# Forgetting attention: the forget sums of the row maxima, subtracted on VectorE inside the reduction instead of added by a TensorE pass

## The chip, the core and the metric

One program runs on one core of a Trainium2 chip. The metric is the device time of one execution in microseconds. All inputs and outputs are in device memory. The numbers are f32; matrix products marked fp32r read f32 operands in the rounded form that the kernel makes by a copy ("hi"), with the rest kept in a second tile ("lo").

## The reference, cut to what matters

The program is one inference step of a two-layer decoder (a gated-linear-attention layer, then a forgetting-attention layer) for a prompt of 2048 tokens and eight single-token samples. The change touches the prompt's forgetting attention alone: 16 heads of 64, causal.

```python
f_all = jnp.cumsum(logf, axis=1)                       # F, one value per token and head
...
s = jnp.einsum('bqhd,bkhd->bhqk', q_blk, k_all)        # q already scaled
s = s + fq_blk.transpose(0, 2, 1)[..., None] - f_k[:, :, None, :]
s = jnp.where((kpos[None, :] <= qpos[:, None])[None, None], s, -jnp.inf)
p = jax.nn.softmax(s, axis=-1)
return jnp.einsum('bhqk,bkhd->bqhd', p, v_all)
```

F of the query is the same for all keys of a row and falls out of the softmax. What is needed is q.k - F(key), its maximum over each query's keys, the exponential of the difference, the sum, and the product with V.

## The kernel before

The kernel is a row of phases, each a block in which every engine has its own instruction stream and waits on semaphores; the order on each engine is the order of the code. The phase of the change is `attention_phase` (L1316 to L1906). The phases ahead of it (modulation, projections, linear attention) and behind it (the samples' attention, the output projection) are not touched.

**Work of a pair.** Two heads share the 128 partitions, 64 each, so there are 8 pairs (`PAIRS`); `step(j, u)` is the work of one pair on an engine and `run_steps` (L1453) runs the eight, six of them in a loop whose body holds two. Queries are cut in 4 groups G of 512, keys in 16 tiles of 128.
- *Logits.* For each group G and key tile i there is one unit e, 40 per pair (`exp_units`). TensorE writes keys x queries of both heads into one of two pairs of PSUM banks: hi by hi, hi by lo, lo by hi, and a fourth product of the tiles `k_more` and `q_more`, whose rows add -F of the key and minus the query's maximum (L1631). ScalarE takes the exponential (L1732), GpSimd adds it to the running sum (L1898), TensorE multiplies it by V (`weigh_v`, L1651).
- *Maxima.* They must be known first, so they are made ahead in the other layout, queries x keys: also 40 units per pair, one for each query tile t and block c of up to 512 keys (`maxima`, L1598). Each is a hi by hi product of both heads, 64 rows each, and a second product of the constant tile `pick_f` (ones in the two rows where `k_more` holds -F in two parts) and `k_more`, which adds -F of the key to every row of the sum (L1602). The unit on the diagonal (c = t // 4) also gets two small bf16 products that write the causal mask, and is 128, 256, 384 or 512 wide. VectorE then takes the maximum of both heads by one TENSOR_REDUCE (L1774).
- All maxima units use one pair of banks (`bank_max`), so TensorE may write the next one only when VectorE has read the last (`max_done`, L1596).

**The order.** `slots_of` gives each unit e of a pair its extras: one maxima unit per slot (slots 0 to 15 the last query group of the same pair, slots 16 to 39 the first three groups of the next pair), and at some slots a transposition of q or k (`turn`), the row of maxima (`m_row`), the sums (`sum`, 16 tiny products) or the reciprocal's transposition (`spread`). In a slot TensorE does (`unit`, L1665): the wait and mask of the unit's logits; for a diagonal maxima unit its wait for `max_done` and its mask; the logits; for any other maxima unit its wait; the maxima; V times the exponentials of the unit before; the slot's extra. VectorE has in each slot the maximum, then the extra's part, then in eight slots (`page_at`) one half of the scoring of a cache page of a sample (a multiplication of 1024 columns at L1797, a reduction at L1800). Before the eight steps stand the first 24 maxima of pair 0 (`first_slots`), with two sets of banks in turn.

**The forget sums** are scanned on VectorE once (`forget_sums`, L1833) into `F`, 16 partitions of 2048, split in -F hi and lo, stored to `f_both` and loaded from there per pair into two rows of `k_more` (`load_f`).

Of the kernel before, what the change touches and what calls it, by code (L numbers as in the profile page):

```python
# [11 lines left out]
P = 128  # L12
# [1303 lines left out]
def attention_phase(nc, g):  # L1316
# [11 lines left out]
    maxima_of = lambda G: [("max", t, c) for t in range(R * G, R * G + R) for c in range(G + 1)]  # L1328
    ahead = [f for G in range(NG - 1) for f in maxima_of(G)]
    AHEAD = len(ahead)  # L1330
    max_slots = list(enumerate([(OWN, f) for f in maxima_of(NG - 1)] + [(NEXT, f) for f in ahead]))
# [35 lines left out]
    page_at = (1, 5, 10, 15, 20, 27, 33, 38)  # L1367
    PT = 5
    with ExitStack() as st:
# [6 lines left out]
        pick_f = sb("pick_f", [P, P], F32R)  # L1376
# [7 lines left out]
        o_raw, spread, o = ([sb(f"{n}{s}", [P, NB]) for s in range(2)] for n in ("o_raw", "spread", "o"))  # L1384
# [13 lines left out]
        v_loaded = [sem(f"v_loaded{u}") for u in range(2)]  # L1398
        turn_full, turn_hi, turn_used = sem("turn_full"), sem("turn_hi"), sem("turn_used")
# [65 lines left out]
        clears = [(ones[:, :], 1.0), (zero[:, :], 0.0), (pick_f[:, :].bitcast(F32), 0.0)]  # L1465
        clears += [(pick_f[at:at + 4, :].bitcast(F32), 1.0) for at in (0, HD)]
        clears += [(pick_f[at:at + 2, :].bitcast(F32), 0.0) for at in (0, HD)]
# [4 lines left out]
        with nc.Block() as block:  # L1472
            @block.sync
            def _(sp):
# [13 lines left out]

                def load_q_sample(j, u):
                    sp.dma_start(q_sample[u][:, :], g.q_fox_s[ds(2 * j + u, 1), :].broadcast_to([P, g.D]))\  # L1490
                        .then_inc(q_sample_loaded[u], 16)
# [12 lines left out]
                def store_o(j, u, base, G, n):  # L1504

                    sp.wait_ge(turn_used, base + n + 1 + 1)
                    sp.dma_start(g.o_foxT[ds((2 * j + u) * P, P), G * NB:(G + 1) * NB], o[G % 2][:, :])\
                      .then_inc(o_stored[G % 2], 16)
# [10 lines left out]
                def step(j, u):  # L1519
                    is_more = not is_last(j, u)  # L1520
                    if is_more:
                        nxt = following(j, u)
                        sp.wait_ge(turn_full, before(j, u))
                        load_rows(*nxt)
                        sp.wait_ge(max_full, UN * (2 * j + u) + AHEAD + 1)
                        if is_first(j, u):
                            sp.wait_ge(cleared, len(clears))
                        load_f(*nxt)
                        load_v(*nxt)
                        sp.wait_ge(page_done, PG * (2 * j + u) + 2)  # L1530
                        load_q_sample(*nxt)
                    for e in range(UN + 1):
                        for who, kind, a, b, n in slots_of(j, u)[e]:
                            if kind == "spread":
                                store_o(*whose(who, j, u), before(j, u), a, n)
                            elif kind != "sum":
                                filler(*whose(who, j, u), before(j, u), kind, a, b, n)
                        if e in (page_at[1], page_at[3]):
                            load_page(j, u, 2 + (e == page_at[3]))
                        if is_more and e in (page_at[5], page_at[7]):  # L1540
                            load_page(*nxt, (e == page_at[7]) * 1)
# [9 lines left out]
                sp.wait_ge(sums_stored, 32)  # L1551
# [16 lines left out]
            def _(pe):  # L1568
# [21 lines left out]
                def max_wait(j, u, t, c, n, spare=0):  # L1590
                    h = 2 * j + u
                    if (t, c) == (0, 0):
                        pe.wait_ge(f_loaded, 32 * h + 32)
                    if t % R == 0 and c == 0:
                        pe.wait_ge(turn_hi, 2 * NG * h + 2 * (t // R) + 2)
                    pe.wait_ge(max_done, UN * h + n + 1 - spare)  # L1596

                def maxima(j, u, t, c, at=bank_max):  # L1598
                    w = min(NB, (t + 1) * P - c * NB)
                    keys, diagonal = slice(c * NB, c * NB + w), c == t // R  # L1600
                    two_heads(at, slice(0, w), hi[0][u], hi[1][u], slice(t * P, (t + 1) * P), keys, not diagonal, False)
                    two_heads(at, slice(0, w), pick_f, more[1][u], slice(0, P), keys, False, True).then_inc(max_full, 1)  # L1602
# [15 lines left out]
                def spread_out(j, u, base, G, n):  # L1618
                    pe.wait_ge(spread_ready, NG * (2 * j + u) + G + 1)
                    for r in range(R):  # L1620
                        mm = pe.transpose(bank_turn[:, r * P:(r + 1) * P], spread[G % 2][:, r * P:(r + 1) * P], g.ident[:, :])
                    mm.then_inc(turn_full, 1)

                def logits_wait(j, u, e):
                    h = 2 * j + u
                    G, i = exp_units[e]
                    if i == 0:
# [90 lines left out]
            def _(act):  # L1718
# [35 lines left out]
                act.wait_ge(sums_stored, 32)  # L1754
# [5 lines left out]
            def _(dve):  # L1760
                def filler(j, u, base, kind, a, b, n, at=lambda n: bank_max, turn_at=lambda n: bank_turn):
# [6 lines left out]
                    if kind == "max":  # L1768
                        t, c = a, b
                        w = min(NB, (t + 1) * P - c * NB)  # L1770
                        if t % R == 0 and c == 0:
                            dve.wait_ge(m_ready, NG * h + t // R + 1)
                        dve.wait_ge(max_full, UN * h + n + 1)
                        dve.tensor_reduce(chunk_max[:, :, t % R, c], pair_of(at(n))[:, :, 0:w], AX.X, ALU.max)\  # L1774
                           .then_inc(max_done, 1)
# [27 lines left out]
                def invert(j, u, base, G, n):  # L1803
# [4 lines left out]
                    dve.tensor_copy(spread[s][:, :].rearrange("p (r d) -> p r d", d=HD),  # L1808
                                    share[s][:, :].unsqueeze(2).broadcast_to([P, 2 * R, HD])).then_inc(spread_ready, 1)

                def finish(j, u, base, G, n):
# [3 lines left out]
                    dve.wait_ge(o_stored[s], 16 * (NG // 2 * h + G // 2) + 16)  # L1815
                    dve.tensor_tensor(o[s][:, :], o_raw[s][:, :], bank_turn, ALU.mult).then_inc(turn_used, 1)
# [470 lines left out]
def build(nc, inp, out):  # L2287

    with ExitStack() as ctx:
# [45 lines left out]
        g.f_both = dram("f_both", (2 * g.HB, T))  # L2335
# [80 lines left out]
```

## Time and profile before

| | us |
|---|---|
| three runs, median (lowest to highest) | 3606.91 (3602.55 to 3608.69) |
| the profiled execution | 3614.84 |
| its span, first to last instruction | 3613.2 |
| PE, DVE, ACT, POOL busy in the span | 3219.0, 1509.1, 968.7, 775.1 |

Times in the rows are microseconds from the start of the span unless marked ns. PE is TensorE's matrix product, PEld its weight load, DVE is VectorE, ACT ScalarE, POOL GpSimd, SPq the queue of SyncE. A timeline row gives start, length, engine, line, output and input, shape, count, and in brackets the idle time in front and what ended it. The two products of a pair of heads lie on different halves of the array and run side by side, so they stand as one row "x2", and the distance from one row's start to the next is what a pair costs. The attention phase lies between about 2284 and 3320 us.

### The profile page before, as it was taken

What the parts mean: (1) busy time and instruction counts of PE and PEld (TensorE: products, weight loads), DVE (VectorE), ACT (ScalarE), POOL (GpSimd) and SP (SyncE); (2) the same over time, 40 slices, a digit from 0 to 9 for tenths busy, and PEclk for the clock granted to TensorE, in tenths of its full rate; (3) what the DMA queues carried; (4) which work ended last, traced back from release to release, by engine and by line L of the source; (5) the groups of instructions that cost most, each with busy time, mean ns of one, the idle gap of its engine ahead of it and who ended that gap; (6) DMA issues with size and microseconds to landing.
All of it is one profiled execution on the core that took longest, in us unless ns stands there. A gap on an engine that the chain in (4) does not pass through costs nothing. (4 is left out here: it accounts for less than half of the span.)

```text
span 3613.2 us, 45740 instructions
## 1 busy us (share of the span) xinstructions
PE 3219.0 (89%) x17364; PEld 2347.2 (65%) x17364; DVE 1509.1 (42%) x2532; ACT 968.7 (27%) x1540; POOL 775.1 (21%) x430
## 2 busy tenths in 40 slices
PE   5599999995999549999959999799999999997599
PEld 2378877884888338888948888555555555553287
DVE  1622222105776364421174401455555555552343
ACT  0412222213544041200552211033333333332100
POOL 1300000000000040000040000256665666667000
PEclk8599999996999659999559999699999999998799
DMA  9411121114444431111041111122202220202733
GB/s 344 134 73 71 70 76 53 71 50 140 140 141 127 164 118 67 70 70 44 8 143 46 69 68 44 51 80 69 68 21 68 70 65 31 69 28 80 281 129 140
DMA packets 211353, 329.64 MB, mean 91 GB/s; under 512 B 23148, under 2 KB 106092, under 8 KB 211089
## 3 DMA queue, kind: packets, MB, share of 16 engines
q1 hardware_dynamic: 208804, 318.86, 25.8%
q0 software_dynamic: 2304, 8.39, 0.6%
q8 instruction: 109, 1.79, 0.2%
q14 instruction: 64, 0.52, 0.0%
q10 hardware_dynamic: 72, 0.07, 0.0%
HBM read 233.41 MB, written 93.61 MB: 91 GB/s over the span
## 5 line engine op out<-in xcount | busy, mean ns | idle before, releaser
L1898 POOL TENSOR_TENSOR at_p_sum<-at_p_sum,at_p 128x1024 f32<-128x1024 f32 (+3 forms) x264 | 535.7, 2029 | 192.7 <-ACT at_p L1732 185.7
L1774 DVE TENSOR_REDUCE at_chunk_max<-psum 128x2 f32<-128x1024 f32 (+2 forms) x320 | 340.1, 1065 | 275.8 <-PE psum L1578 275.3
L1732 ACT ACTIVATE at_p<-psum 128x1024 f32<-128x1024 f32 (+1 forms) x320 | 286.7, 896 | 563.7 <-PE psum L1578 563.7
L1651 PE MATMUL psum<-at_p,at_v 128*64 128x512 f32 (+3 forms) x1280 | 311.0, 567 | 0.1
L806 POOL TENSOR_TENSOR kv_h_lo<-kv_stage,kv_h_hi 128x1024 f32 x16 | 37.7, 2354 | 1128.0 <-ACT kv_h_hi L588 1127.0
L514 PE MATMUL psum<-kv_w_hi,kv_h_hi 128*128 128x512 f32 (+1 forms) x640 | 245.2, 383 | 7.1 <-DVE kv_w_lo L700 7.1
L515 PE MATMUL psum<-kv_w_lo,kv_h_hi 128*128 128x512 f32 (+1 forms) x640 | 244.9, 383 | 0.0
L516 PE MATMUL psum<-kv_w_hi,kv_h_lo 128*128 128x512 f32 (+1 forms) x640 | 244.9, 383 | 0.0
L514 PE MATMUL psum<-gla_w_hi,gla_h_hi 128*128 128x512 f32 x512 | 201.0, 393 | 0.0
L515 PE MATMUL psum<-gla_w_lo,gla_h_hi 128*128 128x512 f32 x512 | 200.0, 391 | 0.0
L516 PE MATMUL psum<-gla_w_hi,gla_h_lo 128*128 128x512 f32 x512 | 199.7, 390 | 0.0
L514 PEld LDWEIGHTS psum<-kv_w_hi,kv_h_hi 128*128 128x128 f32 x640 | 137.4, 215 | 27.4 <-DVE kv_w_lo L700 7.2
L1578 PE MATMUL psum<-at_qT_hi,at_kT_hi 64*128 64x512 f32 (+3 forms) x640 | 153.8, 477 | 0.0
L516 PEld LDWEIGHTS psum<-kv_w_hi,kv_h_lo 128*128 128x128 f32 x640 | 137.4, 215 | 20.3
L515 PEld LDWEIGHTS psum<-kv_w_lo,kv_h_hi 128*128 128x128 f32 x640 | 137.5, 215 | 20.2
L806 POOL TENSOR_TENSOR fox_h_lo<-fox_stage,fox_h_hi 128x1024 f32 x16 | 37.6, 2351 | 493.3 <-ACT fox_h_hi L588 492.2
L2198 PE MATMUL psum<-out_w_hi,out_og_hi 128*128 128x512 f32 x272 | 107.1, 394 | 30.8 <-DVE out_og_lo L2254 30.8
L1578 PE MATMUL psum<-at_kT_hi,at_qT_hi 64*128 64x512 f32 (+3 forms) x640 | 129.3, 400 | 2.0 <-DVE at_chunk_max L1774 1.8
L1651 PEld LDWEIGHTS psum<-at_p,at_v 128*64 128x64 f32 x1280 | 65.5, 138 | 99.8 <-issue 88.4
L1578 PE MATMUL psum<-at_k_more,at_pick_f 64*128 64x512 f32 (+3 forms) x640 | 125.1, 386 | 0.0
L1578 PE MATMUL psum<-at_q_more,at_k_more 64*128 64x512 f32 (+3 forms) x640 | 121.9, 377 | 0.0
L1578 PE MATMUL psum<-at_qT_lo,at_kT_hi 64*128 64x512 f32 (+3 forms) x640 | 121.4, 376 | 0.0
(416 smaller groups left out, 6647.9 us busy)
## 6 DMA issues: line engine op xcount, KB each, us to landing
mod_w<-in_ada_w SPq DMA_DIRECT2D x12, 2048.0 KB, 19.6
at_page<-in_cache_k SPq DMA_DIRECT2D x32, 512.0 KB, 3.5
gla_w_raw<-in_gla_w_in SPq DMA_DIRECT2D x6, 2048.0 KB, 8.3
mod_w<-in_kv_ada_w SPq DMA_DIRECT2D x4, 2048.0 KB, 12.1
v_gla<-gla_stage SPq DMA_DIRECT2D x32, 256.0 KB, 2.0
sg_gla<-gla_stage SPq DMA_DIRECT2D x32, 256.0 KB, 2.0
gl_sg<-sg_gla SPq DMA_DIRECT2D x16, 512.0 KB, 3.7
gl_v<-v_gla SPq DMA_DIRECT2D x16, 512.0 KB
```

Source lines behind the costliest of these rows:

```text
L514: pe.matmul(out, left[0], right[0], start=first, stop=False)
L515: pe.matmul(out, left[0], right[1], start=False, stop=False)
L516: return pe.matmul(out, left[1], right[0], start=False, stop=last)
L806: pool.tensor_tensor(h_lo[:, :, ds(t * P, P)], f_tile[u % 2].rearrange("p (k c) -> p k c", c=P), h_hi[:, :, ds(t * P, P)].bitcast(F32), AL ...
L1578: mm = pe.matmul(bank(bank_at + a)[:, cols], left[half[a], l_cols], right[half[a], r_cols], start=first, stop=last, skip_group_check=True)
L1651: mm = pe.matmul(bank_o[half[a], skip:NB], v[u][:, i, half[a]], p_tile[e % PT][:, a, skip:NB], start=(i == 0), stop=(i == R * G + R - 1), ...
L1732: act.activation(p_tile[e % PT][:, :, skip:NB], pair_of(bank_st[e % 2])[:, :, skip:NB], ACT.Exp)\
L1774: dve.tensor_reduce(chunk_max[:, :, t % R, c], pair_of(at(n))[:, :, 0:w], AX.X, ALU.max)\
L1898: pool.tensor_tensor(p_sum[s][:, :, skip:NB], p_sum[s][:, :, skip:NB], p_tile[e % PT][:, :, skip:NB], ALU.add).then_inc(p_added, 1)
L2198: pe.matmul(ps_y[u][a][:, :], left[0], w_hi[:, k, cols], start=(k == 0), stop=False)
```

## The change

The `pick_f` product of each maxima unit goes, and the tile with it; the hi by hi product now closes the bank. VectorE takes, per head, one `tensor_tensor_reduce`: PSUM minus a tile `f_wide`, written back to PSUM, with the maximum over the columns as accumulator output. `f_wide` holds F of the pair's two heads, the same on all partitions, 2 x 2048 columns. In front of the two a one-column copy into `max_seen` carries the waits. The F rows are stored once to device memory and each pair's are loaded in four blocks of 512 keys (`load_f_wide`, 512 KB each) while the pair before runs. For that each column block must be free early, so the last group's maxima are walked block by block of keys, in place of query tile by query tile. To make room, `o` and `spread` have one buffer each in place of two. The wait for `k_more`'s rows moves from the first maxima unit to the first logits.

```diff
     ahead = [f for G in range(NG - 1) for f in maxima_of(G)]
+    last_maxima = [("max", t, c) for c in range(NG) for t in range(T // P - R, T // P)]
-    max_slots = list(enumerate([(OWN, f) for f in maxima_of(NG - 1)] + [(NEXT, f) for f in ahead]))
+    max_slots = list(enumerate([(OWN, f) for f in last_maxima] + [(NEXT, f) for f in ahead]))
+    f_slots = (R, 2 * R, 3 * R, 4 * R)
...
-        pick_f = sb("pick_f", [P, P], F32R)
+        f_wide = sb("f_wide", [P, 2, T])
+        max_seen = sb("max_seen", [P, UN])
-        o_raw, spread, o = ([sb(f"{n}{s}", [P, NB]) for s in range(2)] for n in ("o_raw", "spread", "o"))
+        o_raw = [sb(f"o_raw{s}", [P, NB]) for s in range(2)]
+        spread, o = sb("spread", [P, NB]), sb("o", [P, NB])
...
+                def load_f_wide(j, u, c):
+                    sp.dma_start(f_wide[:, :, c * NB:(c + 1) * NB],
+                                 g.F[ds(2 * (2 * j + u), 2), c * NB:(c + 1) * NB].rearrange("(o a) t -> o a t", o=1)
+                                 .broadcast_to([P, 2, NB])).then_inc(f_wide_loaded[c], 16)
...
+                        if is_more and e in f_slots:
+                            sp.wait_ge(max_done, UN * (2 * j + u) + AHEAD + R * f_slots.index(e) + R + 1)
+                            load_f_wide(*nxt, f_slots.index(e))
...
-                sp.wait_ge(sums_stored, 32)
+                sp.dma_start(g.F, F.rearrange("p t c -> p (t c)")).then_inc(sums_stored, 16)
+                sp.wait_ge(sums_stored, 48)
+                for c in range(NG):
+                    load_f_wide(0, 0, c)
...
-                    two_heads(at, slice(0, w), hi[0][u], hi[1][u], slice(t * P, (t + 1) * P), keys, not diagonal, False)
-                    two_heads(at, slice(0, w), pick_f, more[1][u], slice(0, P), keys, False, True).then_inc(max_full, 1)
+                    two_heads(at, slice(0, w), hi[0][u], hi[1][u], slice(t * P, (t + 1) * P), keys, not diagonal, True)\
+                        .then_inc(max_full, 1)
...
-                        dve.tensor_reduce(chunk_max[:, :, t % R, c], pair_of(at(n))[:, :, 0:w], AX.X, ALU.max)\
-                           .then_inc(max_done, 1)
+                        dve.wait_ge(f_wide_loaded[c], 16 * h + 16)
+                        dve.tensor_copy(max_seen[:, n:n + 1], g.one[:, :])
+                        for a in range(2):
+                            op = dve.tensor_tensor_reduce(pair_of(at(n))[:, a, 0:w], pair_of(at(n))[:, a, 0:w], f_wide[:, a, c * NB:c * NB + w],
+                                                          1.0, -3.0e38, ALU.subtract, ALU.max, chunk_max[:, a, t % R, c:c + 1])
+                        op.then_inc(max_done, 1)
```

How it stands on the engines. VectorE, the first two slots of the loop body (ISA without a tile is a wait; REGISTER_ALU computes a wait's number). Before:

```order
L1774 TENSOR_REDUCE at_chunk_max<-psum 128x2
L1773 REGISTER_ALU
L1774 TENSOR_REDUCE at_chunk_max<-psum 128x2
L1794 ISA
L1796 ISA
L1797 TENSOR_TENSOR at_page<-at_page,at_q_sample 128x1024
```

VectorE at the same place after the change:

```order
L1790 COPY at_max_seen<-one 128x1
L1792 ISA psum,at_chunk_max<-psum,at_f_wide 128x512
L1792 ISA at_chunk_max 128x1
L1792 ISA psum,at_chunk_max<-psum,at_f_wide 128x512
L1792 ISA at_chunk_max 128x1
L1788 REGISTER_ALU
L1790 COPY at_max_seen<-one 128x1
L1792 ISA psum,at_chunk_max<-psum,at_f_wide 128x512
```

One instruction on both heads becomes five: the copy and, for each head, the subtraction with its maximum and a separate one-column instruction that writes the accumulator out.

TensorE, slot 3 of the loop body (the fourth unit of group 0, with the maxima unit that goes with it). Before:

```order
L1572 MATMUL psum<-hide_qk,ident 128x128 x2
L1578 MATMUL psum<-at_qT_hi,at_kT_hi 128x128 x2
L1578 MATMUL psum<-at_qT_lo,at_kT_hi 128x128 x2
L1578 MATMUL psum<-at_qT_hi,at_kT_lo 128x128 x2
L1578 MATMUL psum<-at_q_more,at_k_more 128x128 x2
L1578 MATMUL psum<-at_kT_hi,at_qT_hi 128x128 x2
L1578 MATMUL psum<-at_k_more,at_pick_f 128x128 x2
```

TensorE in slot 3 after the change:

```order
L1587 MATMUL psum<-hide_kq,ident 128x128 x2
L1593 MATMUL psum<-at_qT_hi,at_kT_hi 128x128 x2
L1593 MATMUL psum<-at_qT_lo,at_kT_hi 128x128 x2
L1593 MATMUL psum<-at_qT_hi,at_kT_lo 128x128 x2
L1593 MATMUL psum<-at_q_more,at_k_more 128x128 x2
L1609 REGISTER_ALU
L1593 MATMUL psum<-at_kT_hi,at_qT_hi 128x512 x2
```

The `pick_f` product is gone, and slot 3 has a full block of 512 keys in place of a diagonal one of 128, whose mask and wait stood ahead of the logits: the last group's four diagonal units moved from slots 3, 7, 11 and 15 to slots 12 to 15.

## Rows read from the trace of the kernel before

**Rows 1.** Busy time, granted clock and DMA share of two stretches
```profile
core 0: us, PE busy (x) PEld busy (x) DVE busy (x) ACT busy (x) POOL busy (x), PEclk, DMA share, GB/s
2350.00:3260.00 910.00, 873.75 (x6092) 489.02 (x6090) 502.03 (x587) 315.15 (x383) 559.56 (x274) 0.96 0.18 57
2311.00:2350.00 39.00, 32.88 (x162) 17.74 (x160) 29.42 (x39) 5.09 (x8) 0.20 (x1) 0.63 0.01 2
```

**Rows 2.** TensorE's waits between 2350 and 3300: total us, times, longest
```profile
PE psum L1572 <- DVE at_chunk_max L1774: 21.0, 51, 1.6
PE psum L1607 <- DVE at_m L1779: 5.6, 7, 0.8
PE psum L1578 <- DVE at_chunk_max L1774: 1.3, 5, 0.3
```

**Rows 3.** Timeline of one whole slot, TensorE and VectorE
```profile
2733.70 0.50 PE L1578 MATMUL psum<-at_qT_hi,at_kT_hi 64*128 64x512 f32 x2
...
2734.74 0.39 PE L1578 MATMUL psum<-at_kT_hi,at_qT_hi 64*128 64x512 f32 x2
...
2734.97 0.39 PE L1578 MATMUL psum<-at_k_more,at_pick_f 64*128 64x512 f32 x2
...
2735.29 1.08 PE L1651 MATMUL psum<-at_p,at_v 128*64 128x512 f32 x4
...
2735.40 1.23 DVE L1774 TENSOR_REDUCE at_chunk_max<-psum 128x2 f32<-128x1024 f32 x1 [0.23 <-PE psum L1578]
...
2736.30 0.94 PE L1614 MATMUL psum<-at_ones,at_p_sum 128*128 128x1 f32 x7
```

**Rows 4.** Timeline of two narrower maxima units, 384 and 256 columns
```profile
2665.02 0.34 PE L1578 MATMUL psum<-at_kT_hi,at_qT_hi 64*128 64x384 f32 x2
2665.20 0.34 PE L1578 MATMUL psum<-at_k_more,at_pick_f 64*128 64x384 f32 x2
...
2691.75 0.28 PE L1578 MATMUL psum<-at_kT_hi,at_qT_hi 64*128 64x256 f32 x2
2691.87 0.28 PE L1578 MATMUL psum<-at_k_more,at_pick_f 64*128 64x256 f32 x2
```

**Rows 5.** Groups by shape, 2311 to 3300: count, busy us, mean ns, idle before
```profile
L1774 DVE TENSOR_REDUCE at_chunk_max<-psum 128x2 f32<-128x1024 f32 x224 | 274.2, 1225 | 210.7 <-PE psum L1578 210.5
L1797 DVE TENSOR_TENSOR at_page<-at_page,at_q_sample 128x1024 f32<-128x1024 f32 x32 | 62.9, 1966 | 1.3 <-DMA at_page<-in_cache_k 1.3
L1800 DVE TENSOR_REDUCE scores<-at_page 128x1024 f32 x24 | 29.1, 1215 | 0.0
L1774 DVE TENSOR_REDUCE at_chunk_max<-psum 128x2 f32<-128x256 f32 x32 | 13.5, 423 | 19.8 <-PE psum L1578 19.8
L1766 DVE TENSOR_TENSOR at_kT_lo<-psum,at_kT_hi 128x512 fp32r<-128x512 f32 x31 | 21.4, 692 | 32.6 <-ACT at_kT_hi L1723 32.6
```

**Rows 6.** Timeline of VectorE, back-to-back and small instructions
```profile
2309.36 0.69 DVE L1766 TENSOR_TENSOR at_qT_lo<-psum,at_qT_hi 128x512 fp32r<-128x512 f32 x1 [6.88 <-ACT at_qT_hi L1723]
2309.97 0.68 DVE L1766 TENSOR_TENSOR at_kT_lo<-psum,at_kT_hi 128x512 fp32r<-128x512 f32 x1
...
2338.45 5.76 DVE L1774 TENSOR_REDUCE at_chunk_max<-psum 128x2 f32<-128x1024 f32 x5
...
3256.43 0.18 DVE L1779 TENSOR_REDUCE at_m<-at_chunk_max 128x8 f32<-128x32 f32 x1
3256.54 1.21 DVE L1800 TENSOR_REDUCE scores<-at_page 128x16 f32<-128x1024 f32 x1
```

**Rows 7.** Timeline of a diagonal unit behind a full one
```profile
2680.58 1.08 PE L1651 MATMUL psum<-at_p,at_v 128*64 128x512 f32 x4
2680.69 1.23 DVE L1774 TENSOR_REDUCE at_chunk_max<-psum 128x2 f32<-128x1024 f32 x1 [0.78 <-PE psum L1578]
2681.97 0.29 PE L1572 MATMUL psum<-hide_qk,ident 128*128 128x128 bf16 x2 [0.32 <-DVE at_chunk_max L1774]
```

**Rows 8.** Timeline of the phase's start: the scan's last step and the F stores
```profile
2300.21 2.28 DVE L1852 SCALAR_TENSOR_TENSOR at_qT_lo<-at_v,at_qT_hi 16x2048 fp32r<-16x2048 f32 x1
...
2304.34 0.42 SPq L1550 DMA_DIRECT2D f_both<-at_qT_lo  x1
...
2308.74 0.60 ACT L1723 ACTIVATE at_qT_hi<-psum 128x512 fp32r<-128x512 f32 x1 [27.11 <-DMA f_both<-at_qT_lo]
```

More of the change, by code:

```diff
@@ L1398, in attention_phase @@
         v_loaded = [sem(f"v_loaded{u}") for u in range(2)]
+        f_wide_loaded = [sem(f"f_wide_loaded{c}") for c in range(NG)]
+        max_chain = sem("max_chain")
         turn_full, turn_hi, turn_used = sem("turn_full"), sem("turn_hi"), sem("turn_used")
@@ L1464, in more_clears @@
                    [(more[b][u][rows_, :].bitcast(F32), 1.0) for b in range(2) for rows_ in (slice(0, 4), slice(HD, HD + 4))]
-        clears = [(ones[:, :], 1.0), (zero[:, :], 0.0), (pick_f[:, :].bitcast(F32), 0.0)]
-        clears += [(pick_f[at:at + 4, :].bitcast(F32), 1.0) for at in (0, HD)]
-        clears += [(pick_f[at:at + 2, :].bitcast(F32), 0.0) for at in (0, HD)]
+        clears = [(ones[:, :], 1.0), (zero[:, :], 0.0)]
         clears += more_clears(0)
@@ L1506, in store_o @@
                     sp.wait_ge(turn_used, base + n + 1 + 1)
-                    sp.dma_start(g.o_foxT[ds((2 * j + u) * P, P), G * NB:(G + 1) * NB], o[G % 2][:, :])\
+                    sp.dma_start(g.o_foxT[ds((2 * j + u) * P, P), G * NB:(G + 1) * NB], o[:, :])\
                       .then_inc(o_stored[G % 2], 16)
@@ L1620, in spread_out @@
                     for r in range(R):
-                        mm = pe.transpose(bank_turn[:, r * P:(r + 1) * P], spread[G % 2][:, r * P:(r + 1) * P], g.ident[:, :])
+                        mm = pe.transpose(bank_turn[:, r * P:(r + 1) * P], spread[:, r * P:(r + 1) * P], g.ident[:, :])
                     mm.then_inc(turn_full, 1)
@@ L1626, in logits_wait @@
                     G, i = exp_units[e]
+                    if e == 0:
+                        pe.wait_ge(f_loaded, 32 * h + 32)
                     if i == 0:
@@ L1753, in _ @@
                 act.sem_inc(o_copied, 1)
-                act.wait_ge(sums_stored, 32)
+                act.wait_ge(sums_stored, 48)
                 for who, kind, a, b, n in first_slots:
@@ L1807, in invert @@
                     dve.wait_ge(turn_used, base + n + 1 + 1)
-                    dve.tensor_copy(spread[s][:, :].rearrange("p (r d) -> p r d", d=HD),
+                    dve.tensor_copy(spread[:, :].rearrange("p (r d) -> p r d", d=HD),
                                     share[s][:, :].unsqueeze(2).broadcast_to([P, 2 * R, HD])).then_inc(spread_ready, 1)
@@ L1814, in finish @@
                     dve.wait_ge(o_copied, NG * h + G + 1 + 1)
-                    dve.wait_ge(o_stored[s], 16 * (NG // 2 * h + G // 2) + 16)
-                    dve.tensor_tensor(o[s][:, :], o_raw[s][:, :], bank_turn, ALU.mult).then_inc(turn_used, 1)
+                    dve.wait_ge(o_stored[1 - s], 16 * (NG // 2 * h + (G + 1) // 2) + 16)
+                    dve.tensor_tensor(o[:, :], o_raw[s][:, :], bank_turn, ALU.mult).then_inc(turn_used, 1)
                 def turn_op(j, u, base, kind, a, b, n):
@@ L2334, in build @@
         g.q_fox, g.sg_foxT, g.o_foxT = dram("q_fox", (T, D)), dram("sg_foxT", (D, T)), dram("o_foxT", (D, T))
-        g.f_both = dram("f_both", (2 * g.HB, T))
+        g.f_both, g.F = dram("f_both", (2 * g.HB, T)), dram("F", (g.HB, T))
         g.k_rows, g.v_rows = (a[0].rearrange("t h d -> t (h d)") for a in (out.k_prompt, out.v_prompt))
```

2 lines of the change are left out of this document (removed).

## The prediction

> **What bounds the kernel now.** The change touches one phase, so I read first the busy times of its stretch, then TensorE's waits, then the timeline of single slots. Between 2350 and 3260 us TensorE is busy 873.75 of 910 us at a granted clock of 0.96, VectorE 502, GpSimd 560, ScalarE 315 [rows 1]. So TensorE sets the pace: a microsecond taken from its stream is a microsecond gained, as long as nothing else comes late. The one partner that already comes late at times is VectorE: TensorE waits 21.0 us in 51 places at the mask of a diagonal maxima unit, 1.3 us at other maxima and 5.6 us for the row of maxima [rows 2]. The timeline shows why. All maxima share one pair of banks. In a full slot VectorE starts on the maxima at 2735.40 and needs 1.23 us, while TensorE spends 1.01 us on V (2735.29 to 2736.30) [rows 3]. If the next maxima unit is a plain one, the logits (2733.70 to 2734.74, 1.04 us) stand in between as well, and the answer is there in time. If it is diagonal, its wait stands ahead of the logits, and TensorE is held 0.32 us [rows 7]. So the question is how much later VectorE's answer comes, and how much of the gain that eats.
>
> **The change part by part.**
>
> *Removed from TensorE.* From the start of the hi by hi pair to the start of the `pick_f` pair are 0.23 us at 512 columns [rows 3], 0.18 at 384 and 0.12 at 256 [rows 4]; I take 0.10 at 128. The next row's distance, 0.32, is longer by a changeover to V that stays. Of 320 units 24 lie in the start, 296 in the eight steps: 209 of 512 and 29 of each narrower width. 209 x 0.23 + 29 x 0.40 = 60 us at full clock, 62 at the mean clock of 0.96. That is the whole gain on offer, if no wait grew.
>
> *Added on VectorE.* One reduction of 1024 columns every 1.152 us (5.76 us for five) [rows 6], answering after 1.23, becomes five instructions. For the subtraction with maximum the nearest row is a tensor_tensor that reads PSUM and SBUF, 512 columns: 692 ns [rows 5], the next one starting 0.61 us later [rows 6]. For the copy and the two accumulator reads the nearest row is a tiny reduction: 0.18 us long, but the next instruction starts 0.11 after it [rows 6]. No row shows an accumulator read, nor VectorE writing to PSUM. Bounds for a read: 0.05 (below the tiny one, since it has no input) and 0.21 (the tiny one's whole length and a little more, if the pipe must be empty first). I take 0.13, a little over the nearest row, because it follows at once on the instruction whose result it needs. A full unit then takes 0.11 + 2 x (0.61 + 0.13) = 1.59 us and answers after 1.67: 0.44 later than now. VectorE's load grows by about 0.4 us per slot, from 55 to some 70% of the stretch, so it doesn't bound by load; it bounds by lateness.
>
> *Waits at diagonal units.* After V about 0.95 us have gone since VectorE's start [rows 7], so a diagonal unit right behind a full one waits 1.28 - 0.95 = 0.33 now and 1.72 - 0.95 = 0.77 then, less what the slot in front has as an extra on TensorE (a sum 1.8, transpositions 0.5). By the slot table seven units of a pair wait 0.33 now: 2.3 us a pair, 17 us over the 7.4 pairs' worth of units, against 21.0 in the trace [rows 2], so the account holds. Then: six wait 0.77 (slots 16, 21, 23, 25, 30, 39), three 0.27 behind a transposition (12, 33, 36), and the rest, behind narrow units or sums, nothing: 5.4 us a pair, 40 in all. Growth: 23 us. The new order spares the last group's diagonal units all but one of these waits, which is counted.
>
> *Waits at plain units.* The room for a plain answer is 0.95 + 1.04, so 1.67 alone fits. It no longer fits where VectorE has more to do. Four page multiplications a pair take 1.97 us and four reductions 1.21 [rows 5]. Now 1.15 + 1.9 overruns a slot of 2.60 by 0.45, within the slack; then 1.59 + 1.9 overruns a slot of 2.37 by 1.1 against a slack of 0.3: 0.8 us four times a pair, 3.2, and some 0.3 for the reductions: 26 us in all. Also, the last units of each group are narrow and their slots last only 1.5 to 1.8 us on TensorE, as slots 1 to 3 do, and the new order puts full blocks there: two waits of about 0.2 in each of four groups, 12 us.
>
> *Start.* In the first 24 maxima TensorE runs at 0.63 and VectorE is busy 29.4 of 39 us [rows 1], with waits both ways. VectorE gets 15 x 0.44 + 9 x 0.4 = 10 us more, TensorE about 8 less at half clock; half of it shows: 5 us. Ahead of it ScalarE waits for the F stores, the second issued at 2304.34 and the wait ended at 2308.74 [rows 8]. A third store behind them adds its issue, 0.4, and VectorE's first maximum waits for `f_wide`: 1 us. Start: +6.
>
> *Hidden.* The `f_wide` loads are issued 12 slots (over 25 us) ahead of their first use, on a DMA system busy to 0.18 [rows 1]; SyncE's new waits name maxima of slots already past, so stores and page loads behind them are held by under a slot. One `o` and one `spread` are free again after a store, with at least two slots in between. The f_both wait moves later. All at 0; if a load came late it would be a microsecond or two a pair.
>
> *Sum.* -62 + 23 + 26 + 12 + 6 = +5 us. Against the profiled 3614.84 that is 3620; the median of the runs lies 8 lower, so 3612. Each 0.1 us more on a full unit stretches all of these waits, 9 at diagonals, 4 at page work and 8 in short slots, 21 a pair: 21 x 7.4 x 0.1 = 16 us.
>
> *A rule beside a row.* The last step of the scan reads two SBUF operands of f32 and takes 2.28 us for 2048 columns [rows 8], which is one column per 0.96 GHz cycle and 0.15. The Trainium skill, "Vector Engine (DVE) Microarchitecture Reference", section "Points that are easy to get wrong", says that this class of instruction with two non-bf16 SBUF sources halves throughput, no port being left for the accumulator. The row disagrees for one without accumulator, and here one source is PSUM; the sum would be by it what the last rival says.
>
> **The rivals.**
> *A, the small instructions are nearly free.* With reads of 0.05 to 0.08 a full unit takes 1.43 to 1.5, and the sum is 5 - 16 x (0.9 to 1.6) = -20 to -9: 3587 to 3598. For it: VectorE starts the next instruction before the last is over [rows 6]. Against it: a dependent read.
> *B, every instruction pays its whole length.* Then a unit is 0.18 + 2 x (0.69 + 0.18) = 1.92 to 2.1 us, the plain units begin to wait as well, and the sum is 5 + 16 x 3.3 = +58 to +80: 3665 to 3687. It ends slower from 1.65 us a unit on. For it: results pass from each subtraction to a read. Against: the starts at 0.61 and 0.11. The Trainium skill, "VectorE: DVE Perf Modes", section "The DRAIN you can't avoid", says that the next op doesn't start until the pipe is empty; the rows of 0.61 don't bear that out for plain instructions.
> *C, the subtraction runs at half rate,* because PSUM is read and written back in the same bank, or for want of a port. 512 columns then take 1.07 + 0.08, a unit 2.7 us, over the slot of 2.37: VectorE is the bound, and the result is 3607 + 296 x 0.5 + what collides, some 3780. No row shows a write to PSUM.
> *D, the clock falls.* Its lower level, 1.2 of 2.4 GHz, is what the 0.63 of the start is mixed from, where TensorE was idle before, and the steps' 0.96 has a little of it too [rows 1]. More waits could bring more: one 3 us spell more in each pair would cost 1.5 us of it, 12 us in all, 3624.
>
> **How the numbers follow.** A measurement of this kernel can tell about 0.2% from no change, 7 us. Forecast case, a unit of 1.5 to 1.7 us: 0.51, times 3598 to 3630, centre 3612. It gives faster 0.06, same 0.26, slower 0.19. A: 0.22, nearly all faster (0.20), the rest same. B: 0.17, C: 0.07, D: 0.03, all slower. Together faster 0.26, same 0.28, slower 0.46. The range leaves out C and the ends of A and B: 3582 to 3680. Both signs hold much of the chance; the forecast case's own range is 3598 to 3630.
>
> **What would show it.** In the changed profile: the distance from maxima pair to V of about 0.32 with nothing between; the full unit on VectorE, first copy to last read, at 1.6 us, its subtraction at 0.69 and its read starting 0.61 behind; TensorE's waits for `chunk_max` at about 85 us in place of 22, most at diagonal units and behind the page work; no wait for `f_wide` beyond the first. TensorE busy in the phase falls by about 60. I am wrong if the unit is under 1.5 or over 1.7, if the waits grow far more or less than the 60 us at a unit of 1.6, or if a load or a lone buffer shows among the waits.

## The result and the profile after

The changed kernel is faster: 3584.56 us against 3607.59, median of 20 runs of each, ratio 0.9942 with a 95% interval of 0.9928 to 0.9955, so 21 us less (16 to 26). The prediction had 3612 in the middle of a range from 3582 to 3680 and gave "slower" 0.46 against 0.26 for "faster": the time lies just inside the range, and the direction was missed. The profiled execution has a span of 3584.9 us against 3613.2.

The stretch of the eight steps, and the start ahead of it, as busy times; the start is the first row, the steps are the second, in which TensorE is idle for some 60 us of 885 [rows 1]. The granted clock of the start is 0.50 where it was 0.63, that of the steps is 0.96 as before:

```profile
core 0: us, PE busy (x) PEld busy (x) DVE busy (x) ACT busy (x) POOL busy (x), PEclk, DMA share, GB/s
2311.00:2350.00 39.00, 27.06 (x102) 13.15 (x102) 34.10 (x135) 5.61 (x9) 0.00 (x0) 0.50 0.20 56
2350.00:3235.00 885.00, 823.19 (x5530) 441.53 (x5530) 571.02 (x1776) 316.16 (x385) 569.12 (x275) 0.96 0.26 76
```

TensorE's waits in the steps (total us, times, longest), which answer [rows 2]:

```profile
PE psum L1587 <- DVE at_chunk_max L1792: 39.3, 58, 1.8
PE psum L1620 <- DVE at_m L1798: 9.1, 8, 1.8
PE psum L1593 <- DVE at_chunk_max L1792: 4.9, 13, 1.1
```

L1587 is the diagonal mask: 39.3 in place of 21.0. The plain units wait 4.9 in place of 1.3, the row of maxima 9.1 in place of 5.6. VectorE's lateness has grown by 25 us in all, and the pass that went was worth more.

The line that decides is VectorE's timeline of one full unit, which answers [rows 3] and [rows 6]:

```profile
2734.20 0.40 PE L1593 MATMUL psum<-at_kT_hi,at_qT_hi 64*128 64x512 f32 x2
...
2734.53 1.08 PE L1666 MATMUL psum<-at_p,at_v 128*64 128x512 f32 x4
2734.64 0.15 DVE L1790 COPY at_max_seen<-one 128x1 f32<-128x1 f32 x1 [0.56 <-PE psum L1593]
2734.71 0.69 DVE L1792 CUSTOM_DVE_ANT_0 psum<-psum,at_f_wide 128x512 f32<-128x512 f32 x1
2735.32 0.14 DVE L1792 DVE_READ_ACCUMULATOR2_ANT at_chunk_max<- 128x1 f32 x1
2735.32 0.73 DVE L1792 CUSTOM_DVE_ANT_0 psum<-psum,at_f_wide 128x512 f32<-128x512 f32 x1
...
2735.96 0.14 DVE L1792 DVE_READ_ACCUMULATOR2_ANT at_chunk_max<- 128x1 f32 x1
```

The subtraction with maximum has the 0.69 us that was taken from the nearest row. But the read of the accumulator and the second subtraction carry the same start, 2735.32: the first read delays nothing. So it is in all 320 units of this profile. The second read delays nothing behind it either (a multiplication starts together with one at 2744.22, shown further down), and it ends 0.05 us after its own subtraction (2736.10 against 2736.05), which is all that it adds to the answer. From copy to the end of the last read (2734.64 to 2736.10) are 1.46 us, where the prediction had 1.67 and the reduction before took 1.23. By shape, the groups that answer [rows 5]:

```profile
L1792 DVE CUSTOM_DVE_ANT_0 psum<-psum,at_f_wide 128x512 f32<-128x512 f32 x448 | 299.6, 710 | 0.0
L1792 DVE DVE_READ_ACCUMULATOR2_ANT at_chunk_max<- 128x1 f32 x640 | 90.3, 141 | 0.0
L1816 DVE TENSOR_TENSOR at_page<-at_page,at_q_sample 128x1024 f32<-128x1024 f32 x32 | 62.6, 1958 | 1.2 <-DMA at_page<-in_cache_k 1.2
```

A reader of these rows alone would add 90.3 us of reads to VectorE's work; the timeline shows that they run beside it.

The phase's start, which answers [rows 8]: stores, `f_wide` loads and the first maximum.

```profile
2305.86 0.43 SPq L1563 DMA_DIRECT2D F<-at_v  x1
...
2310.66 3.15 SPq L1494 DMA_DIRECT2D at_f_wide<-F  x4
2310.66 0.60 ACT L1738 ACTIVATE at_qT_hi<-psum 128x512 fp32r<-128x512 f32 x1 [28.92 <-DMA F<-at_v]
...
2316.56 0.15 DVE L1790 COPY at_max_seen<-one 128x1 f32<-128x1 f32 x1 [2.05 <-DMA at_f_wide<-F]
```

ScalarE starts 1.9 us later than before and the first maximum waits 2.05 us for its load. The first exponential of the steps comes at 2353.47 in place of 2349.78, so the start lost 3.7 us in this pair of profiles, of 6 expected. The steps, from there to the first transposition of the samples' phase (3294.96 here, 3323.30 before), last 941.5 us in place of 973.5.

### The profile page after: what moved, and what is told of

Its sections match the earlier page's. It is cut to its first block and busy times, and to the rows that moved or that the text cites. A ratio compares the mean times of both kernels' runs of the same rounds, so it can differ in the third digit from the quotient of the medians.

```text
span 3584.9 us, 46131 instructions
## 1 busy us (share of the span) xinstructions
PE 3158.7 (88%) x16724; PEld 2299.0 (64%) x16724; DVE 1581.0 (44%) x3812; ACT 968.2 (27%) x1540; POOL 780.7 (22%) x425
## 3 DMA queue, kind: packets, MB, share of 16 engines
q1 hardware_dynamic: 217540, 335.77, 27.9%
## 5 line engine op out<-in xcount | busy, mean ns | idle before, releaser
L1792 DVE CUSTOM_DVE_ANT_0 psum<-psum,at_f_wide 128x512 f32<-128x512 f32 (+3 forms) x640 | 376.8, 630 | 0.0
L1790 DVE COPY at_max_seen<-one 128x1 f32<-128x1 f32 x320 | 48.6, 152 | 211.8 <-PE psum L1593 207.2
L1666 PEld LDWEIGHTS psum<-at_p,at_v 128*64 128x64 f32 x1280 | 65.6, 138 | 97.7 <-issue 90.3
L1593 PE MATMUL psum<-at_qT_hi,at_kT_lo 64*128 64x512 f32 (+3 forms) x640 | 121.3, 375 | 0.0
```

Of the source, the lines that this page charges most:

```text
L1593: mm = pe.matmul(bank(bank_at + a)[:, cols], left[half[a], l_cols], right[half[a], r_cols], start=first, stop=last, skip_group_check=True)
L1666: mm = pe.matmul(bank_o[half[a], skip:NB], v[u][:, i, half[a]], p_tile[e % PT][:, a, skip:NB], start=(i == 0), stop=(i == R * G + R - 1), ...
L1792: op = dve.tensor_tensor_reduce(pair_of(at(n))[:, a, 0:w], pair_of(at(n))[:, a, 0:w], f_wide[:, a, c * NB:c * NB + w], 1.0, -3.0e38, ALU.s ...
```

## The experiments

Twelve runs in three groups, each group on one chip beside the kernel before. What is compared is the ratio to that kernel, which I also give in us of 3607. The length of the steps in one profile is a weaker measure: the changed kernel profiled a second time took 928.0 us for them in place of 941.5, at a mean granted clock of 0.97 in place of 0.95.

```profile
2355.83:3283.83 928.00, 855.83 (x5832) 458.10 (x5831) 580.01 (x1783) 337.02 (x408) 614.76 (x297) 0.97 0.25 73
```

**x1, zero product.** The pass of TensorE is put back, with a tile of zeros.

```diff
-                    two_heads(at, slice(0, w), hi[0][u], hi[1][u], slice(t * P, (t + 1) * P), keys, not diagonal, True)\
-                        .then_inc(max_full, 1)
+                    two_heads(at, slice(0, w), hi[0][u], hi[1][u], slice(t * P, (t + 1) * P), keys, not diagonal, False)
+                    two_heads(at, slice(0, w), pick_f, more[1][u], slice(0, P), keys, False, True).then_inc(max_full, 1)
```

> The changed kernel with a second product put back into each maxima unit, of a tile of zeros, so that TensorE's stream costs what it did before while VectorE does the new work. Theory (the pass was worth its rows, 60 us, and VectorE's lateness takes back about half): TensorE gets 60 us back, some 5 of it in what are now waits, so 3585 + 55 = 3640, and against the kernel before +30. Rival (the pass was half hidden and VectorE's part costs nothing): against the kernel before 0, about 3610.

Measured: 3637.97 us, ratio 1.0081 (1.0054 to 1.0109), +29 us on the kernel before and 50 more than the changed kernel. The theory had +30 and +55. VectorE's new work, with the new order and the `f_wide` loads that come with it, costs 29 us (19 to 39); the pass alone, beside a late VectorE, is worth 50. TensorE's waits at the diagonal masks are 34.8 us here.

**x2, no product.**

```diff
-                    two_heads(at, slice(0, w), hi[0][u], hi[1][u], slice(t * P, (t + 1) * P), keys, not diagonal, False)
-                    two_heads(at, slice(0, w), pick_f, more[1][u], slice(0, P), keys, False, True).then_inc(max_full, 1)
+                    two_heads(at, slice(0, w), hi[0][u], hi[1][u], slice(t * P, (t + 1) * P), keys, not diagonal, True)\
+                        .then_inc(max_full, 1)
...
-                    dve.tensor_scalar(f_parts[0], flat(F), -1.0, None, ALU.mult).then_inc(sums_made, 1)
+                    dve.tensor_scalar(f_parts[0], flat(F), 0.0, None, ALU.mult).then_inc(sums_made, 1)
...
-                    dve.scalar_tensor_tensor(f_parts[1], flat(F), -1.0, f_parts[0].bitcast(F32), ALU.mult, ALU.subtract)\
+                    dve.scalar_tensor_tensor(f_parts[1], flat(F), 0.0, f_parts[0].bitcast(F32), ALU.mult, ALU.subtract)\
```

> The kernel before without the second product of the maxima units; the forget sums are left out of the logits too (they are stored as zeros), so that the exponentials stay finite. VectorE keeps its one reduction. It gives the whole price of the pass. Theory: 60 us less at full clock and some more waits at the diagonals, so -50 to -60: about 3552. Rival (half of the pass was hidden): -30, about 3578.

Measured: 3558.91 us, ratio 0.9868 (0.9833 to 0.9904), -48 us (-35 to -60). The rival of 30 us lies outside. Of the 48 us the changed kernel keeps 21: the difference, some 27 (about 14 to 40), is what the five instructions in place of one cost, with the new order and the loads. TensorE's busy time in the steps (second number) is 61.5 us less in x2 (second row) than in the kernel before (first row), at the same granted clock:

```profile
2349.78:3323.30 973.52, 927.74 (x6424) 515.63 (x6423) 513.51 (x599) 337.43 (x408) 608.10 (x297) 0.95 0.18 54
2348.80:3264.60 915.80, 866.26 (x5833) 462.96 (x5831) 519.46 (x599) 337.26 (x408) 610.47 (x297) 0.95 0.18 58
```

So the pass itself is 61 us of TensorE's time, and the runs show 13 less (1 to 26). One thing on record goes the same way. Each run lists the granted clock as a mean over the execution, and the span times (1 - clock) is what is lost to the lower of the clock's two levels, 1.2 of 2.4 GHz. On this chip it is 361 us for the kernel before, 354 in x3 and 368 in x1, but 379 in x2 and 380 in x4 (each good to 3 or so). So without the pass some 18 us more are lost, whether VectorE is quick (x2) or late (x4); in the other two groups the changed kernel and its variants lose 5 to 12 us more than the kernel before. That would cover the gap between 61 and 48. That it is the cause is not shown, and where in the execution it lies isn't either.

**x3, order only.**

```diff
+    last_maxima = [("max", t, c) for c in range(NG) for t in range(T // P - R, T // P)]
-    max_slots = list(enumerate([(OWN, f) for f in maxima_of(NG - 1)] + [(NEXT, f) for f in ahead]))
+    max_slots = list(enumerate([(OWN, f) for f in last_maxima] + [(NEXT, f) for f in ahead]))
```

> The kernel before with the last group's maxima walked by blocks of keys, nothing else. Theory: full blocks in the short slots 1 to 3 cost more than the spared waits at the diagonals bring: +5 to +10 us. Rival (the prediction's account of the diagonals alone): -3 us, which can't be told from 0.

Measured: 3604.54 us, ratio 0.9994 (0.9977 to 1.0011), -2 us (-8 to +4). The theory's +5 to +10 lies outside, the rival's -3 can't be told from nothing. The waits at the diagonals are 23.7 us and at plain units 2.2. In the kernel before, the order is worth nothing that can be measured; beside the slower unit it was not tried by itself.

**x4, three more copies.** VectorE's answer is made about as late as the prediction had it.

```diff
                         dve.tensor_copy(max_seen[:, n:n + 1], g.one[:, :])
+                        for extra in range(1, 4):
+                            dve.tensor_copy(max_seen[:, (n + 10 * extra) % UN:(n + 10 * extra) % UN + 1], g.one[:, :])
```

> The changed kernel with three more one-column copies in front of each maxima unit's subtraction, 0.07 us each by the changed kernel's rows, so that VectorE answers 0.21 us later: at 1.67 us, what the prediction took. Theory (the account was right but for the accumulator read): 16 us per 0.1 us, +34 on the changed kernel, 3615 to 3620, near the predicted 3612. Rival (the waits at plain units were invented, only those at the diagonals grow): 9 x 7.4 x 0.21 = +14, about 3599.

Its timeline of one unit:

```profile
2740.79 0.15 DVE L1790 COPY at_max_seen<-one 128x1 f32<-128x1 f32 x1 [1.41 <-PE psum L1593]
2740.86 0.26 DVE L1792 COPY at_max_seen<-one 128x1 f32<-128x1 f32 x3
2741.04 0.69 DVE L1794 CUSTOM_DVE_ANT_0 psum<-psum,at_f_wide 128x512 f32<-128x512 f32 x1
...
2742.29 0.14 DVE L1794 DVE_READ_ACCUMULATOR2_ANT at_chunk_max<- 128x1 f32 x1
```

Three copies cost 0.18 us, and the answer comes after 1.64 us. Measured: 3605.36 us, ratio 0.9996 (0.9977 to 1.0016), -1 us on the kernel before (-8 to +6). So 0.18 us more on each unit take away the whole gain: 20 us, 11 per 0.1 us (about 6 to 16 by the two intervals), with the theory's 16 and the rival's 7 at the two ends. The mean granted clock, 0.895, is that of the changed kernel's 20 runs, so the clock is unlikely to have a part in it. This is the run that settles the miss: with an answer nearly as late as I had assumed (1.64 for 1.67) the kernel is no faster. The unit's length is less well matched, 1.50 us from copy to copy where the prediction had 1.59. Its waits:

```profile
PE psum L1587 <- DVE at_chunk_max L1794: 47.5, 60, 1.7
PE psum L1620 <- DVE at_m L1800: 10.7, 8, 2.1
PE psum L1593 <- DVE at_chunk_max L1794: 10.0, 16, 2.7
```

**y1 and y2, late masks.** In `unit`, on the changed kernel (y1) and on the kernel before (y2):

```diff
-                    for at, t, c, n in maxes:
-                        if c == t // R:
-                            max_wait(*at, t, c, n)
-                            masks(bank_max, t % R * P, g.hide_qk)
                     if e < UN:
                         logits(j, u, e)
                     for at, t, c, n in maxes:
-                        if c != t // R:
-                            max_wait(*at, t, c, n)
+                        max_wait(*at, t, c, n)
+                        if c == t // R:
+                            masks(bank_max, t % R * P, g.hide_qk)
                         maxima(*at, t, c)
```

> The changed kernel with the wait and the mask of a diagonal maxima unit behind the slot's logits, as at the plain units. Theory (39 of 53 us of waits are lateness at the diagonals, and 1.04 us of logits cover it): the waits at the masks fall to a third, -25 to -30 us, about 3557. Rival (the waits only move: VectorE starts later in turn and is itself the bound): no change, 3585.

> The kernel before with the same move. Theory: its waits at the diagonal masks, 21.0 us, go: -15 to -20 us, about 3590. Rival: no change, 3608.

Measured: y1 0.9912 (0.9896 to 0.9928) of the kernel before, -32 us, so 11 better than the changed kernel and not 25 to 30. y2 1.0040 (1.0023 to 1.0056), +14 us, worse than the kernel that it started from. Neither theory nor rival had that. The waits did go as the theory said. TensorE's waits in y1's steps (total us, times, longest):

```profile
PE psum L1593 <- DVE at_chunk_max L1789: 12.7, 20, 1.4
PE psum L1620 <- DVE at_m L1795: 10.2, 8, 1.8
```

And in y2's:

```profile
PE psum L1578 <- DVE at_chunk_max L1771: 4.8, 12, 0.5
PE psum L1572 <- DVE at_chunk_max L1771: 0.4, 1, 0.4
```

So the later place costs TensorE itself something. A unit with a sum ahead of it, first in the kernel before, then in y2 with the mask late; each ends with the start of the next V:

```profile
2736.30 1.95 PE L1614 MATMUL psum<-at_ones,at_p_sum 128*128 128x1 f32 x16
2738.10 0.27 PE L1572 MATMUL psum<-hide_qk,ident 128*128 128x128 bf16 x2
2738.30 0.50 PE L1578 MATMUL psum<-at_qT_hi,at_kT_hi 64*128 64x512 f32 x2
...
2739.34 0.28 PE L1578 MATMUL psum<-at_kT_hi,at_qT_hi 64*128 64x256 f32 x2
2739.45 0.28 PE L1578 MATMUL psum<-at_k_more,at_pick_f 64*128 64x256 f32 x2
2739.66 0.65 PE L1651 MATMUL psum<-at_p,at_v 128*64 128x512 f32 x2
```

```profile
2743.40 1.95 PE L1614 MATMUL psum<-at_ones,at_p_sum 128*128 128x1 f32 x16
2745.27 0.50 PE L1578 MATMUL psum<-at_qT_hi,at_kT_hi 64*128 64x512 f32 x2
...
2746.07 0.40 PE L1578 MATMUL psum<-at_q_more,at_k_more 64*128 64x512 f32 x2
2746.40 0.29 PE L1572 MATMUL psum<-hide_qk,ident 128*128 128x128 bf16 x2
2746.62 0.39 PE L1578 MATMUL psum<-at_kT_hi,at_qT_hi 64*128 64x256 f32 x2
2746.84 0.28 PE L1578 MATMUL psum<-at_k_more,at_pick_f 64*128 64x256 f32 x2
2747.05 0.65 PE L1651 MATMUL psum<-at_p,at_v 128*64 128x512 f32 x2
```

From the sum to V are 3.36 us before and 3.65 in y2, though neither waits. Ahead of the logits, behind the full-array sum, the mask adds 0.13 (sum to logits 2.00 against 1.87). Behind the logits it adds 0.32: the last logits and the maxima are 0.55 us apart in y2, and 0.23 without a mask [rows 3]. The next 64-row pair then comes 0.22 behind the maxima in place of 0.11. Compared slot by slot over all diagonal units, without waits and without the stretches at the lower clock, the way from V to V is 0.08 to 0.31 us longer in y2, most where a sum or a transposition stands ahead. The average is 0.20, which for 116 diagonal units is 23 us.

y2 lost 14 us while its waits fell by 16, so 30 us have to be found. They are these 23 and what is lost to the lower clock, reckoned as at x2: 378 us in place of 366, some 11 more. That is enough, within the noise. That the price comes from changing between 64-row and full-array products is how I read it; no run separates it.

**y3, early F.** F is stored when it is scanned, ahead of its split, and ScalarE's wait for the stores moves behind the first 24 maxima.

```diff
+                sp.wait_ge(sums_made, 3)
+                sp.dma_start(g.F, F.rearrange("p t c -> p (t c)")).then_inc(F_stored, 16)
+                sp.wait_ge(F_stored, 16)
+                for c in range(NG):
+                    load_f_wide(0, 0, c)
                 sp.wait_ge(sums_made, 5)
...
-                act.wait_ge(sums_stored, 48)
                 for who, kind, a, b, n in first_slots:
                     filler(0, 0, 0, kind, a, b, n, first_turn(n))
+                act.wait_ge(sums_stored, 32)
```

> The changed kernel with F stored as soon as it is scanned and its loads issued ahead of the other stores, and ScalarE's wait for the stores behind the first 24 maxima. Theory (the start waits for the loads of f_wide, and those for a store that needn't wait for the hi and lo parts): the first maximum comes 5 to 7 us earlier, -4 to -7 us, about 3579. Rival (TensorE at half clock is the bound of the start): 0.

Measured: 3577.15 us, ratio 0.9903 (0.9887 to 0.9919), -35 us and 14 better than the changed kernel. The first maximum's copy stands at 2304.16 in place of 2316.56:

```profile
2298.33 3.09 SPq L1495 DMA_DIRECT2D at_f_wide<-F  x4
...
2304.16 0.15 DVE L1793 COPY at_max_seen<-one 128x1 f32<-128x1 f32 x1 [0.39 <-DMA at_f_wide<-F]
```

The mechanism is the expected one, the first maximum comes 12.4 us earlier where 5 to 7 were expected, and the gain of 14 us (about 7 to 21) is some twice what was expected.

**y4, late masks and early F.** The edits of y1 and y3 together.

> Late masks and early F together on the changed kernel. Theory: the two lie in different stretches and add up: -30 to -36 us against the changed kernel, about 3551. Rival: as y1 alone.

Measured: 3570.7 us, ratio 0.9887 (0.9871 to 0.9902), -41 us; that is 20 better than the changed kernel, near the sum of what y1 and y3 measured (11 and 14), short of what I had expected of them.

**z0, the changed kernel again.**

> The changed kernel as it is, beside the three others on the same chip, so that they can be compared with it directly. Every theory: 0.994 of the kernel before, some 21 us less.

Measured: 0.9938 (0.9921 to 0.9954), -22 us.

**z1, late masks in nine slots, with early F.**

```diff
+                    late = e in (12, 16, 21, 23, 25, 30, 33, 36, 39)
                     for at, t, c, n in maxes:
-                        if c == t // R:
+                        if c == t // R and not late:
                             max_wait(*at, t, c, n)
                             masks(bank_max, t % R * P, g.hide_qk)
```

> The changed kernel with early F, and with late masks in nine slots a pair only (12, 16, 21, 23, 25, 30, 33, 36, 39), where a diagonal unit comes behind a full one and no sum stands between. Theory (a late mask costs TensorE 0.24 us by the steps of the run with all masks late, and is worth it only where there is a wait): the waits fall as with all masks late, 31 us, at a cost of 9 x 7.4 x 0.24 = 16, so -15 us in the steps and -11 in the start, about 26 less than the changed kernel, 3559. Rival (what costs is not the mask's place but the shorter time VectorE is left with later): as with all masks late, 3570.

Measured: 3562.78 us, ratio 0.9872 (0.9853 to 0.9891), -46 us: the fastest of all, 24 better than z0 beside it, where 26 were expected. The waits at masks and plain units are 3.9 and 14.1 us. Its rival, 3570 as with all masks late, is not excluded: against y4's ratio the intervals overlap, so that nine late masks are better than all is likely but not shown. What is shown is that z1, late masks and early F together, is 24 us (about 15 to 33) better than the changed kernel.

**z2 and z3, page multiplication cut to one column,** in the changed kernel (z2) and in the kernel before (z3).

```diff
-                        dve.tensor_tensor(page[w % 2][:, :], page[w % 2][:, :], q_sample[u][:, :], ALU.mult).then_inc(page_prod, 1)
+                        dve.tensor_tensor(page[w % 2][:, 0:1], page[w % 2][:, 0:1], q_sample[u][:, 0:1], ALU.mult).then_inc(page_prod, 1)
```

> The changed kernel with the page multiplication cut to one column, so that VectorE is free of 32 x 1.8 us; the samples' scores are then not computed rightly. It prices the page term of the prediction. The prediction's account at the unit measured: it should be worth 10 to 15 us. Rival (the multiplications stand behind their slot's own answer and fall where TensorE has other work): 0 to 5 us.

> The same cut in the kernel before, the samples' scores again not computed rightly. Both theories: close to 0, at most 5 us of its 21 us of waits at the diagonals.

Measured: z2 0.9925 (0.9908 to 0.9943), 5 us less than z0 (from 14 less to 4 more); z3 0.9994 (0.9980 to 1.0008). Taking 32 x 1.8 us = 58 us off VectorE brings 5 us at most as a middle value, in the changed kernel, and nothing that can be measured in the one before. z2's waits at the masks are 33.5 us against 39.5 in z0. All three waits for VectorE together are 46.3 us in z2 against 55.5 in z0. The 10 to 15 us that the prediction's account gives at the measured unit are likely too dear, and its lower end is not excluded; whether the multiplications cost 0, 5 or 10 us can't be told.

## Why the prediction was wrong

*What bounds the kernel.* Right. TensorE sets the pace and VectorE is the one that comes late; x4 shows how steep that is.

*The pass removed, 62 us.* Mechanism and size are right for TensorE's own time, 61.5 us less busy in x2. What the execution gains by it is less: 48 us (35 to 60) by x2 and 50 by x1. Of the difference 3 us are longer waits at the diagonals (23.9 us in x2), and the 18 us more at the lower clock would cover the rest; the sum had nothing for the clock.

*The new unit on VectorE, 1.59 us and an answer after 1.67.* This is the step that failed: the term "accumulator read". Subtraction and its spacing (0.69, 0.61) were read from the nearest row and are right to 0.03. The copy costs 0.07 in place of 0.11. The accumulator read was taken at 0.13, between bounds of 0.05 and 0.21, and it takes no time from what follows: the first read and the next subtraction start together, which takes 0.13 off the answer, and the last read lasts 0.14 where I had 0.21. The true value lay below my lower bound. I had reasoned that a read must follow what it reads and so comes at a price; it does follow it, but delays nothing behind it. The unit lasts 1.32 us, copy to copy, and answers after 1.46. At the slope of x4, 0.21 us less are 23 us (13 to 34): the whole distance between 3612 and 3585 but for 4, and with it the direction.

*Waits at diagonals, growth 23 us.* Measured +18 at 1.46 and +26 at 1.64 (x4: 47.5 against 21.0). So about right in size, a little small at the unit that it was made for. The count by slots, which gave 17 us for the waits before against 21.0, was a fair instrument.

*Waits at plain units, growth 38 us.* Wrong by a factor. They grew by 3.6 us, and in x4, near the assumed unit, by 8.7; the wait for the row of maxima, for which the sum had nothing, grew by 3.5 and 5.1 beside them. A multiplication stands behind its slot's own maximum, so it delays the next slot's; and behind slots 1, 10 and 20 the next slot has a sum or a transposition on TensorE. The changed kernel's slots 10 to 12:

```profile
2744.22 1.35 DVE L1816 TENSOR_TENSOR at_page<-at_page,at_q_sample 128x1024 f32<-128x1024 f32 x1
...
2745.43 0.66 PE L1602 MATMUL psum<-ident,at_k_rows 128*128 128x128 f32 x4
2745.49 0.14 DVE L1790 COPY at_max_seen<-one 128x1 f32<-128x1 f32 x1
...
2747.00 0.29 PE L1587 MATMUL psum<-hide_qk,ident 128*128 128x128 bf16 x2 [0.91 <-DVE at_chunk_max L1792]
```

The multiplication makes the maximum start late, TensorE transposes meanwhile, and what is left is a wait at the next diagonal mask, 0.91 us. I had counted this case twice, once as page work and once as a diagonal.

*Errors that cancelled.* At the assumed unit the sum said +5 us and x4 measured -1 (-8 to +6). That agreement is luck. By x4's rows all waits for VectorE grew by 40 us, from 27.9 to 68.2, where the sum had 61; and the sum left out the lower clock, some 19 in x4's group. The total held, and its parts didn't.

*Start, +6.* Measured +3.7 in one pair of profiles, with the third store, a wait of 2.05 us for `f_wide`, and a clock of 0.50 in place of 0.63. The first exponential comes at 2348.8 to 2353.1 in the profiles of x2, x3 and z3, which have the old reduction, and at 2347.9 to 2355.8 in those of x4, y1, z0 and z2, which have the new unit, so the size is not firm.

*Hidden parts.* Right: TensorE and VectorE have no wait for `f_wide` but the first, none for `o` or `spread` beyond one of 0.8 us.

*The rivals.* A is what happened, though it had only 0.22, and the measured time lies at the lower end of its 3587 to 3598, since it still paid 0.05 for a read. B fell: in the unit shown above every instruction starts before the last one ends. By the Trainium skill, "VectorE: DVE Perf Modes", section "The DRAIN you can't avoid", the next op waits until the pipe is empty, but one that is not held starts earlier. The rows agree with the second half, which the prediction left out. C (the "last rival" of the prediction's rule beside a row) fell with the 0.69 us for 512 columns, read from and written back to the same PSUM bank. The Trainium skill, "Vector Engine (DVE) Microarchitecture Reference", section "Points that are easy to get wrong", halves the throughput for two such sources in SBUF; with one source in PSUM the runs show no halving.

D has something in it, which the steps' clock (0.96 as before) hides: over the whole execution 18 to 19 us more are lost to the lower clock in x2 and x4, and 9 in z0, than in the kernel before beside them. But D's cause, more waits, is not enough: x2 has the quick reduction and loses as much as x4, and x1 has the late VectorE and loses 7. The missing pass is what x2 and x4 share; yet y2, which has it, loses 11 more too, so it is not the only thing that moves the clock.

*Slips in the sums.* By the prediction's own slope a unit of 2.1 us gives +87, not +80, and the kernel turns slower at 1.60 us a unit, not 1.65. C's 0.5 us for each of 296 units has no source: 2.7 less the slot of 2.37 is 0.3. None of them moves the middle of the forecast.

## What to carry to other kernels

Where one engine waits for another through a single buffer, the price of a change is the answer's delay, not the busy time added: 90 us of reads delayed nothing here, and 0.18 us of copies per unit cost the whole gain. When two engines trade work, look first for waits that stand earlier in the waiting engine's stream than they must, and weigh against them what the move costs: it won 11 us where the waits were long (y1) and lost 14 where they were short (y2). That moving only the late ones is better still is likely (z1), and not shown. When no row shows an instruction, the lower bound of its price is zero, not a little under the shortest row. And time taken off the busiest engine need not all come back: here 61 us of TensorE's work gave 48.

## What the runs showed of the hardware

An accumulator read of 0.14 us has the same start as the subtraction behind it, in all 320 units of the changed kernel's profile, and doesn't delay it; the subtraction then shows 0.73 us in place of 0.69. One-column copies follow each other every 0.06 to 0.07 us though each row says 0.15. VectorE's in-place subtraction in PSUM, with a second operand from SBUF, takes 0.69 us for 512 columns, as one that writes to SBUF does, and narrow ones 311 ns for 128. On TensorE a 128-column bf16 mask of two banks takes 0.11 us beside another mask and 0.20 to 0.22 from its start to that of the logits; between two 64-row products it adds 0.32, and the pair behind the maxima comes 0.1 us later still. With the pass of 61 us taken out the granted clock, as the mean of an execution, was 0.894 (x2) against 0.900 for the kernel before on the same chip; with the late VectorE but the pass put back it was 0.899 (x1). And the same kernel's steps took 941.5 and 928.0 us in two executions, with mean granted clocks of 0.95 and 0.97: single profiles of this kernel can't settle less than about 15 us.
